# Both MLP projections of a one-core decoder layer by one level of Strassen's scheme

## What is computed

```python
hid = jnp.square(jax.nn.relu(rmsnorm(h, norm_mlp_g[l]) @ w_up[l]))   # 2048 -> 8192
h = h + hid @ w_down[l]                                              # 8192 -> 2048
y = rmsnorm(h, final_norm_g)
```

## Time and profile before

| | |
|---|---|
| three runs | 2352.52, 2350.08, 2352.28 us; median 2352.28 |
| profiled execution, first to last instruction (span) | 2349.0 us |
| what the three runs lie above that span, by their median | 3.3 us |
| matmuls (and weight loads) recorded | 16932 (16932) |
| DMA traffic | 204.47 MB, mean 87 GB/s |

### The profile page before, as it was taken

The page is one execution under the profiler, slowest core; times in us unless marked ns, Lnnn a source line. Parts: engine busy times, 40 slices in busy tenths (PEclk is TensorE's granted clock), DMA queues, the critical chain, the costliest instruction groups (busy, mean ns, idle before and its releaser), DMA issues.

```text
span 2349.0 us, 42574 instructions
## 1 busy us (share of the span) xinstructions
PE 2291.0 (98%) x16932; PEld 2263.7 (96%) x16932; DVE 686.9 (29%) x826; ACT 570.3 (24%) x717; POOL 966.5 (41%) x504
## 2 busy tenths in 40 slices
PE   6899999899999999999999999999999999999996
PEld 6899999699999999999999999999999999999996
DVE  6667610832243212211221221122123112212314
ACT  4444411632232211211211221122112112112231
POOL 6344433645544333333333333333333333333354
PEclk8999999999999999999999999999999999999998
DMA  5322242132222222222222222222222222222222
GB/s 168 83 76 85 87 144 84 70 126 86 84 72 87 83 81 81 81 89 81 80 80 84 86 80 80 80 86 83 80 80 82 88 81 80 80 83 87 81 81 90
DMA packets 64245, 204.47 MB, mean 87 GB/s; under 512 B 7040, under 2 KB 15656, under 8 KB 63912
## 3 DMA queue, kind: packets, MB, share of 16 engines
q1 hardware_dynamic: 56544, 190.55, 24.5%
q10 hardware_dynamic: 7656, 13.27, 2.1%
HBM read 196.97 MB, written 8.80 MB: 88 GB/s over the span
## 4 chain that ended last, share of the span: by engine, by line
PE 94%; DVE 3%; POOL 1%; issue 1%; ACT 0%; DMA 0%; DVEq 0%; SPq 0%; ACTq 0%; POOLq 0%
PE ps L440 91%; PE ps L701 1%; PE ps L488 1%; DVE h_res L1595 1%; DVE stat L1463 0%; DVE probs L1462 0%; PE ps L466 0%; POOL w_lo L1067 0%; DVE act_lo L1543 0%; DMA w_raw<-weights 0%; PE ps L475 0%; DVE stat L1464 0%; POOL spt L1091 0%; POOL spt L1092 0%; DVE xc L1362 0%
## 5 line engine op out<-in xcount | busy, mean ns | idle before, releaser
L1067 POOL TENSOR_TENSOR w_lo<-w_raw,w_hi 128x1024 fp32r<-128x1024 f32 x343 | 835.1, 2436 | 1214.9 <-ACT w_hi L753 1209.6
L440 PE MATMUL ps<-act_hi,w_hi 128*128 128x288 f32 (+1 forms) x3456 | 748.8, 298 | 21.8 <-DVE act_lo L1327 9.8
L440 PE MATMUL ps<-act_lo,w_hi 128*128 128x288 f32 (+1 forms) x3456 | 746.7, 298 | 0.0
L753 ACT ACTIVATE w_hi<-w_raw 128x1024 fp32r<-128x1024 f32 x344 | 363.6, 1060 | 1570.1 <-PE ps L440 1500.0
L440 PE MATMUL ps<-act_hi,w_lo 128*128 128x288 f32 (+1 forms) x3456 | 739.6, 295 | 0.0
L440 PEld LDWEIGHTS ps<-act_hi,w_hi 128*128 128x128 f32 x3456 | 558.6, 189 | 25.4 <-issue 11.8
L440 PEld LDWEIGHTS ps<-act_lo,w_hi 128*128 128x128 f32 x3456 | 559.0, 189 | 0.0
L440 PEld LDWEIGHTS ps<-act_hi,w_lo 128*128 128x128 f32 x3456 | 557.2, 189 | 0.0
L440 PE MATMUL ps<-hid_lo,w_hi 128*128 128x288 f32 x1984 | 426.6, 296 | 0.0
L440 PE MATMUL ps<-hid_hi,w_hi 128*128 128x288 f32 x1984 | 424.4, 294 | 0.0
L440 PE MATMUL ps<-hid_hi,w_lo 128*128 128x288 f32 x1984 | 422.1, 294 | 0.0
(11 more groups left out here) (186 smaller groups left out, 882.1 us busy)
## 6 DMA issues: line engine op xcount, KB each, us to landing
w_raw<-weights SPq DMA_DIRECT2D x344, 512.0 KB, 3.3
x_raw<-x_t SPq DMA_DIRECT2D x8, 592.0 KB, 9.3
h_res<-x_t ACTq DMA_DIRECT2D x4, 1152.0 KB, 9.7
y_t<-h_res SPq DMA_DIRECT2D x8, 288.0 KB, 3.0
gy_dram<-gy ACTq DMA_DIRECT2D x1, 1536.0 KB
y_t<-y_part SPq DMA_DIRECT2D x2, 720.0 KB, 4.3
gate_w<-w_gates ACTq DMA_DIRECT2D x8, 128.0 KB, 2.1
bias_p<-gy_dram ACTq DMA_DIRECT2D x1, 1024.0 KB
```

The costliest lines, as they stand in the source:

```text
L440: ins = nc.tensor.matmul(ps[:, 2 * buf + half, 0:width], w, act[:, kk, c0 + half * width:c0 + (half + 1) * width], start=first and part == ...
L753: nc.scalar.activation(w_hi[:, slot, :, :], w_raw[:, slot % RAW, :].rearrange("p (k n) -> p k n", k=SLAB_K), ACT.Copy).then_inc(hi_ready, 1)
L1067: nc.gpsimd.tensor_tensor(w_lo[:, slot, :, :], w_raw[:, slot % RAW, :].rearrange("p (k n) -> p k n", k=SLAB_K), w_hi[:, slot, :, :].bitcas ...
```

## The change

Both projections are done by one level of Strassen's scheme in Winograd's form. A pair of feature tiles and the two token halves make a 2 x 2 block of activations (a quad); a pair of input and a pair of output feature tiles make a 2 x 2 block of weights. Seven products of sums of such blocks take the place of eight. All sums (of weights, of activations, of products) are made in float32, and each operand of a product is split in `hi` and `lo` as before, so a product is still three matmuls, now of one half of 288 tokens each.

The MLP is 71 units in line: 32 of the up projection (one for each pair of hidden tiles, 8 quads of input) and 39 of the down projection. The down units go in a skewed order: unit 32+t covers output pair t mod 8 and hidden quads t-7 to t as far as they exist, so 8 output pairs are visited in turn, each visit adding up to 8 quads. Units with t of 0 to 6 have 1 to 7 quads, those with t of 32 to 38 have 7 to 1.

- Squares of the hidden layer are stored to DRAM (`store_hid`) and read back when the down units reach them (`hid_load`). The running sum of an output pair, 4 x 288 columns, is read from DRAM (`base_load`), four of its blocks are copied into PSUM banks 1, 2, 5, 6 by ScalarE (`seed`), the products accumulate onto them without a start flag, and the result is stored again (`store_sum`). The residual `h` itself goes to DRAM first (`store_h`).
- A ring of 9 quads in SBUF holds `hi` and `lo` of seven activation operands each. ScalarE makes `hi`, VectorE differences and `lo`.
- Weights come in 4 blocks a unit (512 KB each for 8 quads) into six slots (`w_load`). VectorE forms four sums in place (`w_sum`) and all rests (`w_rest`); ScalarE rounds (`w_round`) into three slots. GpSimd takes no part in the MLP's weights any more.
- The seven products of a unit have a PSUM bank each; VectorE combines them with 6 or 7 additions of 288 columns and ScalarE copies two of them.
- The final norm's squares are taken at the last units (`fin_square`), and the output is in another layout, undone on the host.

The core of the diff (sizes, SP's, TensorE's, ScalarE's and VectorE's lists):

```diff
+UP = D_FF // (2 * P)                  # 32
+DEPTH = KT // 2                       # 8
+DOWN = UP + DEPTH - 1                 # 39
+TILES2 = UP + DOWN
+def window(v):
+    if v < UP:
+        return list(range(DEPTH))
+    t = v - UP
+    return list(range(max(0, t - DEPTH + 1), min(t + 1, UP)))
+X_OPERAND = [0, 1, 2, 5, 4, 3, 6]
+SEEDED = [1, 2, 5, 6]
+W_FREED = [5, 6, 7, 3]
...
+        def w_load(v, b):
+            if v >= TILES2:
+                return
+            g = 4 * v + b
+            if g >= 6:
+                vo, bo = divmod(g - 6, 4)
+                sp.wait_ge(wl_ready, 7 * vo + W_FREED[bo])
...
+            sp.dma_start(w_block(v, b), w_mlp[at:at + n].rearrange("(p n) -> p n", p=P)).then_inc(blk_landed[g % 6], 16)
...
+        def base_load(v):
+            t = v - UP
+            if t < DEPTH:
+                sp.wait_ge(h_stored, 48 * DEPTH)
+            else:
+                sp.wait_ge(home_stored[HOME[v - DEPTH]], 16 * (stores_before(v - DEPTH) + 1))
+            if HOME[v] < 2:
+                sp.wait_ge(home_stored[HOME[v]], 16 * stores_before(v))
+            sp.dma_start(home_flat(v), h_dram[t % DEPTH]).then_inc(base_landed[HOME[v]], 16)
...
+        for v in range(TILES2):
+            if v == UP:
+                sp.wait_ge(prod_done, 7 * UP)
+                for t in (1, 2, 3):
+                    base_load(UP + t)
+                hid_load(2)
...
+            if UP < v <= 2 * UP - 1:
+                store_sum(v - 1)
+            w_load(v + 1, 2)
+            if 1 <= v <= UP:
+                store_hid(v - 1)
+            if UP - 1 <= v < 2 * UP and HOME[v + 1] < 2:
+                base_load(v + 1)
+            w_load(v + 1, 3)
...
+            if UP < v < 2 * UP - 2:
+                hid_load(v - UP + 2)
+            w_load(v + 2, 0)
+            w_load(v + 2, 1)
...
+        def unit(v):                                     # TensorE
...
+            for i, x in enumerate(X_OPERAND):
+                bank_free(v, i)
+                pe.wait_ge(wl_ready, 7 * v + i + 1)
+                if i == 0 and v > 0:
+                    pe.wait_ge(quad_lo, newest + 1)
+                if i == 3:
+                    pe.wait_ge(diff_lo, newest + 1)
+                wh, wl = w_half(v, i, 0), w_half(v, i, 1)
+                sow = not (v >= UP and i in SEEDED)
+                for k, j in enumerate(quads):
+                    if i == 0 and v == 0:
+                        pe.wait_ge(quad_lo, j + 1)
+                    slot = quad_at(v, j)
+                    for step, (w, lo) in enumerate(((wh, 0), (wh, 1), (wl, 0))):
+                        ins = nc.tensor.matmul(ps[:, i, 0:HW], w[:, k, :], quad[:, slot, lo, x, :], ...)
+                ins.then_inc(prod_done, 1)
...
+        def w_round(v, i):                               # ScalarE
...
+            o = 7 * v + i
+            if o >= 3:
+                act.wait_ge(prod_done, o - 2)
...
+            nc.scalar.activation(w_half(v, i, 0), w_operand(v, i), ACT.Copy).then_inc(wh_ready, 1)
+        def seed(v, i):
+            k = SEEDED.index(i)
+            if k == 0:
+                act.wait_ge(base_landed[HOME[v]], 16 * loads_upto(v))
+            act.wait_ge(evac, EV[v - 1] + {1: 1, 2: 4, 5: 5, 6: EVACS[v - 1]}[i])
+            nc.scalar.activation(ps[:, i, 0:HW], home(v)[:, {1: 0, 2: 3, 5: 2, 6: 1}[i], :], ACT.Copy,
+                                 scale=1.0 if i in (1, 2) else -1.0).then_inc(seeded, 1)
+        def unit(v):
+            n = quad_formed(v)
+            more = UP <= v + 1 < TILES2
+            act.wait_ge(prod_done, 7 * v + 1)
...
+            nc.scalar.activation(part[:, 0, :], ps[:, 0, 0:HW], ACT.Copy).then_inc(s1_ready, 1)
+            w_round(v, 3)
...
+            w_round(v, 4)
+            if 1 <= v <= UP:
+                act.wait_ge(relu_ready, v)
+                nc.scalar.activation(home(v - 1), home(v - 1), ACT.Square).then_inc(hid_squared, 1)
+            if more:
+                seed(v + 1, 1)
+            if n is not None:
+                quad_high(n)
+            w_round(v, 5)
+            w_round(v, 6)
+            if n is not None:
+                diff_high(n)
+            act.wait_ge(prod_done, 7 * v + 5)
...
+            nc.scalar.activation(part[:, 1, :], ps[:, 4, 0:HW], ACT.Copy, scale=-1.0).then_inc(n5_ready, 1)
+            w_round(v + 1, 0)
+            if more:
+                seed(v + 1, 2)
+            w_round(v + 1, 1)
+            if more:
+                seed(v + 1, 5)
+                seed(v + 1, 6)
+            w_round(v + 1, 2)
...
+        def quad_diff(n):                                # VectorE
+            quad_wait(n)
...
+            v.tensor_tensor(diff[:, 0:2, :], x[:, 0:3:2, :], x[:, 3:4, :].to_broadcast([P, 2, HW]), ALU.subtract)
...
+        def quad_low(n):
+            dve.wait_ge(quad_hi, n + 1)
+            v.tensor_tensor(quad[:, quad_slot(n), 1, 0:3, :], quad_src(n)[:, 0:3, :],
+                            quad[:, quad_slot(n), 0, 0:3, :].bitcast(F32), ALU.subtract).then_inc(quad_lo, 1)
...
+        def w_rest(u, i):
...
+            dve.wait_ge(wh_ready, 7 * u + i + 1)
+            v.tensor_tensor(w_half(u, i, 1), w_operand(u, i), w_half(u, i, 0).bitcast(F32), ALU.subtract).then_inc(wl_ready, 1)
...
+        def unit(u):
...
+            w_rest(u, 3)
+            if 1 <= u <= UP:
+                relu(u - 1)
+            if d is not None:
+                quad_diff(d)
...
+            dve.wait_ge(prod_done, 7 * u + 2)
+            dve.wait_ge(s1_ready, u + 1)
...
+            v.tensor_tensor(c[:, 0, :], bank[1], part[:, 0, :], ALU.add).then_inc(evac, 1)
+            w_rest(u, 4)
+            if n is not None:
+                quad_low(n)
+            w_rest(u, 5)
+            dve.wait_ge(prod_done, 7 * u + 4)
+            v.tensor_tensor(part[:, 2, :], bank[3], part[:, 0, :], ALU.add).then_inc(evac, 1)
+            w_rest(u, 6)
+            if n is not None:
+                diff_low(n)
...
+            dve.wait_ge(n5_ready, u + 1)
+            v.tensor_tensor(part[:, 3, :], part[:, 1, :], part[:, 2, :], ALU.subtract).then_inc(evac, 1)
+            v.tensor_tensor(c[:, 3, :], bank[2], part[:, 1, :], ALU.add).then_inc(evac, 1)
+            w_rest(u + 1, 0)
+            w_sum(u + 1, 0)
+            dve.wait_ge(prod_done, 7 * u + 6)
+            v.tensor_tensor(c[:, 2, :], part[:, 3, :], bank[5], ALU.subtract).then_inc(evac, 1)
+            w_sum(u + 1, 1)
+            w_rest(u + 1, 1)
...
+            dve.wait_ge(prod_done, 7 * u + 7)
+            v.tensor_tensor(c[:, 1, :], part[:, 3, :], bank[6], ALU.subtract).then_inc(evac, 1)
+            w_sum(u + 1, 2)
+            w_rest(u + 1, 2)
+            w_sum(u + 1, 3)
```

More of the change, by code:

```diff
@@ L413, in _ @@
                 raw_load(i, j, True)
[L416 to L427, removed]
@@ L432, in _ @@
+        sp.wait_ge(h_stored, 48 * DEPTH)
+        for b in range(2 + 3):
+            sp.wait_ge(home_stored[b], 16 * sum(HOME[w] == b for w in range(2 * UP - 1)))
+        sp.wait_ge(stored, 16 * (2 + 16 + 3))
     @block.tensor
@@ L476, in spread, with spread_half @@
             ins.then_inc(spread_ready, 1)
+        def spread_half(src, bank):
+            nc.tensor.matmul(ps[:, bank, 0:HW], ones, src, start=True, stop=True).then_inc(spread_ready, 1)
         def xready(k):
@@ L687, in last_tiles @@
[L687 to L735, removed]
@@ new lines, in _, with half_sums @@
+        for v in range(TILES2):
+            unit(v)
+        def half_sums(half, bank):
+            parts = [t[:, 2 * half + b, :] for t in (fin_acc, fin_sq) for b in range(2)]
+            pe.wait_ge(fin_squared, 7 + 2 - half)
+            token_sums(*parts, cols=NORM_HALF[0], bank=bank)
+        pe.wait_ge(fin_added, 6)
+        half_sums(1, 7)
+        pe.wait_ge(evac, EV[TILES2])
+        half_sums(0, 3)
+        for half in (1, 0):
+            pe.wait_ge(diag_ready, 6 - half)
+            for bank in FIN_BANKS[half]:
+                spread_half(fin_diag[:, half, :], bank)
@@ L987, in _ @@
         square_h(1, 1)
+        store_h(0)
+        gain_h(0)
+        quad_high(0)
+        diff_high(0)
         with act.Fori(1, KT // 2 - 1) as j:
@@ L1050, in _ @@
-        for half in range(2):
-            for i in range(LAST):
-                square_part(half * LAST + i)
-            root(4 + half, 3)
+        gain_h(2)
+        square_h(KT - 1, 1)
+        store_h(KT // 2 - 1)
+        quad_high(1)
+        w_round(0, 0)
+        diff_high(1)
+        quad_high(2)
+        for n in range(2, DEPTH):
+            if n + 1 < DEPTH:
+                gain_h(n + 1)
+            diff_high(n)
+            if n == 3:
+                w_round(0, 1)
+            if n == 5:
+                w_round(0, 2)
+            if n + 1 < DEPTH:
+                quad_high(n + 1)
@@ new lines, in _ @@
+        for v in range(TILES2):
+            unit(v)
+            if v >= 2 * UP:
+                fin_square(v - 2 * UP)
+        v = TILES2 - 1
+        act.wait_ge(fin_added, 6)
```

(28 more changed lines are left out.)

607 lines of the change are left out of this document (395 added, 212 removed).

## The result

The changed kernel is slower: 2383.69 us median (2382.94 to 2386.31) against 2351.31 us for the kernel before in the same comparison, a ratio of 1.014, 95% interval 1.0125 to 1.0154. The profiled execution took 2382.94 us, its span is 2380.9 us, 31.9 more than before.

What follows compares the result with a forecast made beforehand. It took TensorE's matmuls, 98% busy, as the bound. Terms -204 + 79 + 1 + 52 + 5 + 15 + 36 + 3 = -13, with +4 for doubt -9: span 2340, forecast 2343 us, range 2270 to 2400.

Steps and rivals of the forecast that it cites:

- Matmuls, -204: In the MLP's products on TensorE: 1536 fewer matmuls, 10752 in all, at 132.8 ns each, -204.0 us.
- Rival 4: In the products: matmuls slower than 132.8 ns because both operands come from new tiles; 3 ns are 32 us, 2375; chance 0.05.
- The steady down units, +79: Down units with 8 quads: VectorE's waits give a 25.6 us period, TensorE idle 3.3 us in each of 24: +79 us.
- The landing: Running-sum read issued behind a 512 KB load in down units: lands 4.7 us after release, bounds 4.0 to 7.1.
- Rival 1: At base_load in 28 down units: the read lands late, 28 us per us, 2410 us at 7.1; chance 0.14.
- Rival 3: In the down units: the wait ring doesn't bind, units take 22.3 us, total 2245 us; chance 0.12.
- the ring: Down units: operand 4's remainder releases load, then read, seed, quad_high; VectorE waits for quad_high, a 6.2 us gap.
- The clock: TensorE stops of some 3 us can bring 1.2 GHz for 4 to 10 us; hidden under VectorE's 25.6 us in down units.
- Rival 2: In each down unit the clock falls, returning after 10 us: 5 us lost, unit 27.4, +45, 2388 us; chance 0.07.
- First down units, unit 31, entry: Units with 1 to 7 quads +52, a late read in unit 31 +5, MLP entry waiting for quads and clock +36 us.
- Last down units, +15: Units with 3 to 1 quads: fin_square ahead of the next first copy, and GpSimd's additions slowing VectorE: +15 us.
- Tail, +3: From last matmul to end: 22.3 us now, about 25 after, with last sum, squares, diagonals, spread and store: +3 us.

Runs made afterwards that it cites:

- e4_sum_first: The changed kernel with VectorE's w_sum 3 moved ahead of the remainder of operand 2: 2353.71 us, ratio 1.0011 to the kernel before.
- e3_read_first: The changed kernel with SP issuing the running-sum read ahead of the 512 KB weight load, still after operand 4: 2348.53 us, ratio 0.9991 to the kernel before.
- e2_seed_late: The changed kernel with ScalarE's first seed moved from ahead of quad_high to behind diff_high: 2244.44 us, ratio 0.9547 to the kernel before.
- e6_fin_later: The kernel with the entry edit, plus fin_square moved behind ScalarE's rounding of the next unit's operand 4: 2214.38 us, ratio 0.9418 to the kernel before.
- e7_pool_off: e6_fin_later with GpSimd's last addition of squares given to VectorE: 2213.92 us, ratio 0.9424 to the kernel before.
- the entry edit: Unit 0's first three products interleaved, added to the changed kernel with early read, late seed and w_sum 3 moved ahead: 2222.17 us, ratio 0.9455.

## Why the prediction was wrong

The forecast was 9 us less than before, and it became 32 more: inside the stated range of 2270 to 2400, but in the other direction.

**Matmuls, -204.** Right: 10752 at 132.7 ns. Rival 4, slower matmuls, is out.

**Up units.** Right: TensorE was without a hole from 748 to 1417 us; the MLP's up half costs its matmuls.

**The steady down units, +79: the step that failed.** The mechanism was right in each of its parts and the runs opened it at two of them. The size was off: 26.74 us a unit, not 25.6. The prediction summed VectorE's queue from operand 5's remainder to the next operand 4 to 17.3 us, as work with small hand-overs. It left out that the remainder of operand 2 waits for a rounding which waits for the sum issued directly before it: the sum ends, ScalarE rounds for 1.06, and VectorE stands 1.19 us in each unit. In the mean of 23 steady units that stretch of the queue took 18.1 us in the changed kernel, and 17.1 with the two lines exchanged (e4_sum_first). That exchange took 30.0 us away and left 25.62 us a unit, the forecast's own number. With this 1.1 us on each of 24 units, and some in the first ones, the sum of the prediction comes out at about +18 us instead of -9 (24 x 1.1 = 26.4, and a little in the first ones), which is slower than before.

**The landing.** Sized well: 4.5 us median from the issue, the seed 5.0 us after the release against 4.8 taken. Rival 1 had the right sign and price, 28 us per us, confirmed by e3_read_first, but not the cause: the gap before `quad_low` was 6.4 us in the mean instead of 6.2, so the landing gave 0.2 us a unit of it.

**Rival 3, that the ring doesn't bind,** was false for this kernel, but its sum was for a kernel without a ring: 2245 us, and e2_seed_late measured 2244.44. That it fits to 1 us is partly luck. Counted as in the table above, that kernel had nothing in unit 31 (5 in the sum), 31 us in the first down units (38), 4 less than at 132.75 ns in the steady ones (0 in the sum), 23 in the last (15) and 9 in the tail (3), and its MLP began 2 us late: the errors cancel. What does carry over is that steady units take TensorE's own time once the ring is open.

**The clock.** The prediction said that a fall in each down unit would be hidden, and also that a clock under 1.00 there would show it wrong. The first holds nearly. Windows of one steady unit of the changed kernel (length, then PE, PEld, DVE, ACT, POOL busy, clock, DMA share, GB/s):

```profile
1657.00:1659.00 2.00, 0.40 (x2) 0.42 (x3) 2.00 (x4) 2.00 (x3) 0.00 (x0) 0.86 0.00 0
1659.00:1661.00 2.00, 2.00 (x10) 2.00 (x10) 2.00 (x2) 1.42 (x3) 0.00 (x0) 0.50 0.79 182
1661.00:1663.00 2.00, 2.00 (x14) 2.00 (x13) 2.00 (x4) 0.42 (x1) 0.00 (x0) 0.79 1.05 410
1663.00:1665.00 2.00, 2.00 (x17) 2.00 (x16) 1.90 (x4) 1.24 (x2) 0.00 (x0) 1.00 0.98 350
```

TensorE stood 3.92 us before 1658.61, the clock was at 1.2 GHz for some 3 us from there, and full again before 1663. That is some 1.5 us lost in this unit, where TensorE had 3 to 4 us to spare. It did not fall in every unit, and in some it stayed low for longer:

```profile
1690.00:1736.00 46.00, 41.63 (x312) 41.19 (x311) 30.82 (x37) 18.20 (x25) 0.00 (x0) 1.00 0.37 142
1737.00:1743.00 6.00, 5.14 (x21) 5.17 (x22) 5.90 (x8) 3.10 (x5) 0.00 (x0) 0.50 0.67 232
```

Over the 23 steady units it fell in 15, around stops of TensorE of 2.3 to 5.3 us, in five of them for some 7 us; in the other eight, with stops of 2.1 to 2.5 us, it stayed at 1.00. The Trainium skill (TensorE: Matmul & The Clock Gate, HAM oscillation) says that a kernel which stalls in a loop is throttled again each time; the trace agrees in those 15 units and not in the other eight. It took little time here, since VectorE's chain set the unit: some 3 us in all, in the five units with the long stretch, where VectorE waited for products. With the clock still falling in about every second unit, e4_sum_first ran at the 25.6 us that take no account of it. Rival 2, a return only after 10 us, did not come about.

**First down units, unit 31, entry.** Right within 3 us each.

**Last down units, +15, measured +22.** The place was named (`fin_square` ahead of the first copy), the price too low: e6_fin_later took 9.6 us back by moving it alone. How much of the 15 was meant for it the prediction doesn't say.

**Tail, +3, measured +9.** Two terms of it were too small. One sum of 288 columns took 2.81 us beside GpSimd's addition instead of the 0.45 that I took; the earlier trace rows show this effect, and I had applied it to the last units but not here. And the sums over features run at half clock (granted clock 0.50 from 2344.6 to 2368.4), 10.37 us for 48 short matmuls in the chain:

```profile
2350.11 2.82 DVE fin_b L1898
...
2353.84 10.37 PE ps L682 x48
```

The large misses pointed the same way: a wait left out or a price taken alone where the operation runs in company.

## What to carry to other kernels

When a wait ring is found in a plan, cut it before you price it: 130 us of this change hung on one read standing behind one wait in SP's queue, or one copy standing ahead of another on ScalarE, and the arithmetic saved was there all the time. In a queue written out by hand, check each instruction for an operand that another engine makes from the result of the instruction just before it, since that round trip (here 1.19 us a unit, most of 30 us) is in no sum of durations. Put such a pair apart by any independent work that is in the queue anyway, and put work that nobody waits for behind the first copy of a unit, not ahead of it.

## What the runs showed of the hardware

- The same 168 matmuls took 22.29 us in the up units and 22.13 in the down units of the changed kernel's siblings. After the entry edit, which changes only unit 0's instructions, the up units take 22.13 too: 31 x 0.16 = 5 us, the rest of that run's 11. In the trace the distances between matmuls in a slow up unit reach 0.145 us once in 48 or 72, in a fast one they are never over 0.140; these few make up only part of the difference. What decides between the two was not tried.
- VectorE's addition of two SBUF tiles started 0.12 us after GpSimd's (2349.99, 2.61 us long) and ended 0.3 us behind it; the same addition took 0.46 us in e7_pool_off, where GpSimd does nothing at that place. An addition with one operand in PSUM is not slowed: in the tail of the changed kernel seven of 576 columns (L1973) took 0.74 to 0.75 us beside GpSimd's, and one without it 0.75. The Trainium skill (SBUF — State Buffer, SBUF: two separate sides) says that the two engines take a shared port pair for a whole instruction, and that a VectorE operation with two SBUF inputs is locked out by a GpSimd one that reads SBUF and started first; the trace agrees.
- A 576 KB read right behind a 512 KB load landed 4.5 us after its issue, and right ahead of one 3.8 us (medians of 30).
